# A hybrid decoder layer on one core: combinations of w_out formed during the input projection, and the down projection split between the two halves

## The chip, the cores and the metric
The kernel runs on one NeuronCore of one Trainium2 chip. A core has a matrix engine (TensorE, PE in the profile), a vector engine (VectorE, DVE), a scalar engine (ScalarE, ACT), GpSimd (POOL) and SyncE (SP), which here issues all the DMAs. Each engine takes its instructions in program order and waits on semaphores. The metric is the device time of the whole program in microseconds.

## The reference
One layer over 2048 positions of width 1024, all in float32. RMS norm, one input projection, stick-breaking attention in 8 heads of 64 beside a gated short convolution, one output projection w_out over both, residual; then RMS norm and SwiGLU with a hidden width of 2816.

```python
h = _rms_norm(x, norm_mix[l])
proj = h @ w_in[l]
q, k, v, cb, cc, cu = jnp.split(proj, splits, axis=-1)
...
mix = jnp.concatenate([attn, conv], axis=-1)
x = x + mix @ w_out[l]
h = _rms_norm(x, norm_ffn[l])
g = h @ w_gate[l]
u = h @ w_up[l]
x = x + (jax.nn.silu(g) * u) @ w_down[l]
```

## The kernel before
Each float32 matmul is made of three in a rounded format: an operand is split into a high part (ScalarE, a rounding copy) and a low part (operand minus high part, on VectorE or GpSimd), and PE does high x high, high x low and low x high.

**Input projection (`qkv_stage`).** 16 tiles of 128 tokens. PE does, per tile t, the 24 matmuls of q, the transposes of the normalized x of tile t+1 (L405) and of q and k of tile t-1 (L415), then k, then v. The root for the norm of tile t+1 is made by GpSimd (`x_rstd`, L222 and L225) at the head of its step t; VectorE scales x with it (L320) at the head of its own. GpSimd's other work in a step is the root for q and k (L236, L239). SyncE ends step t with the store of v (L203), for which it waits on `v_done`, and begins the next with x, then the transposed h. All engines meet at the end of the stage.

**Attention and convolution (`attend_conv_stage`)**, untouched, to about 1102 us.

**The back (`back_stage`)** does w_out, gate, up and down. w_out, gate and up use a Strassen-Winograd scheme: seven products P1 to P7 of blocks in place of eight. For that, operand A (tokens of mix, or weights of gate and up) and operand B (w_out; then h of one half of the tokens) are combined: A's sums on VectorE (`pair_sum`, L1623 to L1639; `sums`, L1701 to L1715), B's four combinations in `t_part` (VectorE, L1692) with one `copy` on ScalarE (L1434). B has seven regions of 1 MB (high and low part 4 x 512 columns each); `b_hi` (L1442) rounds, `b_lo` (L1222) makes the low part, on VectorE or GpSimd by `LO_ON_DVE` and `LO_ON_POOL`.
B is filled three times: with w_out (f = 0), with h of the first 1024 tokens (f = 1), with h of the other 1024 (f = 2), each time as the products before set regions free; `HOME` says which region a product's B is in. A product is 12 matmuls (L1920 to L1924).
The order: the opening (the first two pairs of token tiles, 14 products by the list `OPENING`), six more pairs of seven products (`MIX`); 11 rounds of 14 products (gate and up) for the first half, 11 for the second; then down in 4 groups of 22 chunks, 24 matmuls a chunk (L76 to L78). In a round ScalarE rounds the operands of the next round (`hi`, L1454), keeps results of PE (`keep`, L1472) and does the silu; GpSimd makes the low parts (`lo`, L1873); SyncE loads the next round's raw weights when the last low part of the round before is made (`load_raw`, L1287). The 12 loads of h for f = 2, its combinations and low parts stand in the last round of the first half and the first of the second ("the turn" below). In down, `split` (ScalarE), `wd_split` (VectorE) and `hid_split` (GpSimd) prepare the chunk ahead; down's operands lie in regions of A, its result in `s`, which the rounds use too.
The orders are written out by hand: each engine's block is one list in program order.

Of the kernel before, what the change touches and what calls it, by code (L numbers as in the profile page):

```python
# [110 lines left out]
def qkv_stage(nc, cst, x, norm_mix, w_in, q_norm, k_norm, hT_hi_dram, hT_lo_dram, qk_hi_dram, qk_lo_dram, v_dram):  # L111
# [9 lines left out]
    with ExitStack() as stack:  # L121
# [14 lines left out]
        qkT_hi, qkT_lo = m.sb("qkT_hi", [P, 2, 2 * PAIRS, P], F32R), m.sb("qkT_lo", [P, 2, 2 * PAIRS, P], F32R)  # L136
        proj = m.ps("proj", [P, 2, 3, BANK])
# [13 lines left out]
        v_stored, qkT_stored = [m.sem("v_stored0"), m.sem("v_stored1")], [m.sem("qkT_stored0"), m.sem("qkT_stored1")]  # L151
        block = m.block()
# [21 lines left out]
        def _(sp):
# [35 lines left out]
            tiles(sp, step, tail=3)  # L210
            sp.wait_ge(qkT_lo_done, 2 * TILES)
            store_qk(TILES - 1, (TILES - 1) % 2)
            for b in range(2):
                sp.wait_ge(v_stored[b], DMA * TILES // 2)
                sp.wait_ge(hT_stored[b], DMA * TILES)
                sp.wait_ge(qkT_stored[b], DMA * TILES)

        @block.gpsimd
        def _(pool):
# [22 lines left out]
            tiles(pool, step)  # L242
# [1834 lines left out]
```

## Time and profile before

| | us |
|---|---|
| median of 3 runs | 2678.88 |
| lowest and highest | 2678.44, 2680.89 |
| the profiled execution | 2681.3 |
| its span, first to last instruction | 2679.4 |
| PE busy in the span | 2510.6 |
| VectorE, GpSimd, ScalarE busy | 1349.9, 1321.9, 1164.4 |
| mean granted clock of PE | 0.974 |

The profiled execution's time is 1.9 us more than its span. The stages in it: projection to 322 us, attention and convolution to 1102, w_out from 1119 to 1318, gate and up to 2196, down to the end. A row of the timeline gives start and duration of an instruction (or of a few alike, xN), and in brackets how long its engine stood idle before it and what released it. A matmul's duration contains its pipeline; where they follow each other, the distance of the starts is what one costs.

### The profile page before, as it was taken

How to read it: one execution, taken by the hardware profiler on the slowest of the kernel's cores; microseconds unless marked ns; L12 is line 12 of the kernel's file. 1: busy time of each engine (PE TensorE's matmuls, PEld its weight loads, DVE VectorE, ACT ScalarE, POOL GpSimd, SP SyncE). 2: the span in 40 equal slices, each digit the busy share in tenths (PEclk: the TensorE clock that was granted, in tenths of full speed). 3: DMA queues.
4: the chain of work that ended last, by engine and by line, in shares of the span. 5: the costliest groups of instructions: out<-in, count | busy, mean ns of one | idle time of the engine just before them, and what ended most of it. 6: DMA issues, size and time to landing. Idle time of an engine off the chain costs nothing.

```text
span 2679.4 us, 34937 instructions
## 1 busy us (share of the span) xinstructions
PE 2510.6 (94%) x12176; PEld 2072.5 (77%) x12176; DVE 1349.9 (50%) x1377; ACT 1164.4 (43%) x1883; POOL 1321.9 (49%) x918
## 2 busy tenths in 40 slices
PE   8999779999899999579899999989999999999999
PEld 6788667777777778468778888868888888888887
DVE  4434246766667767465665454574454432222232
ACT  3222256777677677433443333343333322322222
POOL 1212156767667676465684455464455423333332
PEclk9999989999999999789999999989999999999999
DMA  5655563443533522335522222323212225555554
GB/s 173 199 177 166 160 187 99 122 113 98 144 88 103 164 68 53 134 124 206 189 95 94 82 71 82 119 85 95 94 60 84 92 90 171 186 172 183 173 189 153
DMA packets 305117, 343.93 MB, mean 128 GB/s; under 512 B 19169, under 2 KB 242401, under 8 KB 303969
## 3 DMA queue, kind: packets, MB, share of 16 engines
q1 hardware_dynamic: 304992, 342.44, 41.3%
q8 instruction: 58, 0.95, 0.1%
q14 instruction: 67, 0.54, 0.1%
HBM read 243.81 MB, written 98.57 MB: 128 GB/s over the span
## 4 chain that ended last, share of the span: by engine, by line
PE 50%; POOL 2%; DMA 1%; issue 1%; DVE 1%; ACT 1%; DVEq 0%; ACTq 0%; POOLq 0%
PE ffn_ps L1920 11%; PE ffn_ps L1924 11%; PE ffn_ps L1922 11%; PE ffn_ps L77 6%; PE ffn_ps L78 6%; PE ffn_ps L76 6%; POOL all_B L1222 1%; POOL ffn_A L1873 1%; DMA ffn_raw<-in_w_up 1%; DVE all_B_over L1692 0%; DMA ffn_s<-in_x 0%; PE ffn_ps L1950 0%; POOL ffn_A L1856 0%; ACT all_B L1442 0%; ACT ffn_A L1454 0%
## 5 line engine op out<-in xcount | busy, mean ns | idle before, releaser
L1920 PE MATMUL ffn_ps<-all_B,ffn_A 128*128 128x512 f32 x1456 | 576.9, 396 | 64.7 <-issue 18.4
L1924 PE MATMUL ffn_ps<-all_B,ffn_A 128*128 128x512 f32 x1456 | 574.0, 394 | 0.0
L1922 PE MATMUL ffn_ps<-all_B,ffn_A 128*128 128x512 f32 x1456 | 574.0, 394 | 0.0
L1873 POOL TENSOR_TENSOR ffn_A<-ffn_raw,ffn_A 128x512 fp32r<-128x512 f32 x264 | 369.1, 1409 | 379.8 <-ACT ffn_A L1454 379.6
L829 DVE TENSOR_TENSOR_SCAN att_stick<-att_z,att_stick 128x128 f32<-128x128 f32 (+5 forms) x192 | 331.3, 1726 | 220.5 <-ACT att_z L741 209.2
L875 POOL TENSOR_TENSOR att_a<-att_a,att_stick 128x128 f32<-128x128 f32 (+5 forms) x192 | 281.4, 1471 | 217.1 <-DVE att_stick L829 216.5
L1920 PEld LDWEIGHTS ffn_ps<-all_B,ffn_A 128*128 128x128 f32 x1456 | 278.1, 191 | 127.0 <-issue 52.0
L1881 POOL TENSOR_TENSOR ffn_A<-ffn_A_over,ffn_A 128x512 fp32r<-128x512 f32 x88 | 158.3, 1799 | 349.0 <-ACT ffn_A L1494 349.0
L1924 PEld LDWEIGHTS ffn_ps<-all_B,ffn_A 128*128 128x128 f32 x1456 | 277.7, 191 | 58.8
L1922 PEld LDWEIGHTS ffn_ps<-all_B,ffn_A 128*128 128x128 f32 x1456 | 278.1, 191 | 57.4
L1746 DVE TENSOR_TENSOR ffn_A<-ffn_A_over,ffn_A 128x1024 fp32r<-128x1024 f32 x88 | 107.8, 1225 | 348.3 <-ACT ffn_A L1492 348.3
L76 PE MATMUL ffn_ps<-ffn_A 128*128 128x512 f32 x704 | 273.9, 389 | 0.0
L77 PE MATMUL ffn_ps<-ffn_A 128*128 128x512 f32 x704 | 273.9, 389 | 0.0
L78 PE MATMUL ffn_ps<-ffn_A 128*128 128x512 f32 x704 | 273.9, 389 | 0.0
L1454 ACT ACTIVATE ffn_A<-ffn_raw 128x512 fp32r<-128x512 f32 x264 | 162.6, 627 | 235.0 <-PE ffn_ps L1924 88.1
L1492 ACT ACTIVATE ffn_A<-ffn_A_over 128x1024 fp32r<-128x1024 f32 x88 | 93.3, 1060 | 333.4 <-PE ffn_ps L78 326.8
L752 ACT ACTIVATE att_aT_hi<-att_tr 128x512 fp32r<-128x512 f32 (+2 forms) x320 | 158.2, 535 | 148.0 <-PE att_tr L965 146.9
L841 DVE TENSOR_TENSOR att_aT_lo<-att_tr,att_aT_hi 128x512 fp32r<-128x512 f32 (+2 forms) x320 | 180.6, 597 | 34.1 <-ACT att_aT_hi L752 33.4
L965 PE MATMUL att_tr<-all_ident,att_a 128*128 128x128 f32 x1088 | 159.5, 281 | 36.4 <-DVE att_aT_lo L841 33.5
L965 PEld LDWEIGHTS att_tr<-all_ident,att_a 128*128 128x128 f32 x1088 | 128.6, 143 | 76.3 <-issue 33.6
L1472 ACT ACTIVATE ffn_s<-ffn_ps 128x512 f32<-128x512 f32 x132 | 78.5, 596 | 224.9 <-PE ffn_ps L1924 224.8
L76 PE MATMUL att_proj<-att_hT_hi,att_w_hi 128*128 128x512 f32 x384 | 161.5, 421 | 15.3 <-ACT att_y L777 8.5
(118 smaller groups left out, 4676.6 us busy)
## 6 DMA issues: line engine op xcount, KB each, us to landing
ffn_A_over<-in_w_down SPq DMA_DIRECT2D x88, 512.0 KB, 3.5
att_w_stage<-in_w_in SPq DMA_DIRECT2D x48, 512.0 KB, 4.3
ffn_raw<-in_w_gate SPq DMA_DIRECT2D x22, 1024.0 KB, 6.9
ffn_raw<-in_w_up SPq DMA_DIRECT2D x22, 1024.0 KB, 9.0
hidT<-ffn_s SPq DMA_DIRECT2D x88, 256.0 KB, 2.4
ffn_A_over<-hidT SPq DMA_DIRECT2D x88, 256.0 KB, 3.5
qkv_x_t<-in_x SPq DMA_DIRECT2D x16, 512.0 KB, 4.5
hT_hi<-qkv_hT_hi SPq DMA_DIRECT2D x16, 512.0 KB, 5.4
```

What stands on the lines that cost most here:

```text
L76: nc.tensor.matmul(out, lhs_hi, rhs_hi, start=first, stop=False)
L77: nc.tensor.matmul(out, lhs_hi, rhs_lo, start=False, stop=False)
L78: return nc.tensor.matmul(out, lhs_lo, rhs_hi, start=False, stop=last)
L829: nc.vector.tensor_tensor_scan(stick[:, row % 2, c0:c1][:, ::-1], z[:, n % 2, 0:nb * P][:, ::-1], stick[:, row % 2, S:S + 1].to_broadcast( ...
L841: nc.vector.tensor_tensor(aT_lo[:, gi % 2, blocks, toks], tr[:, f % 2, 0:nj, :], aT_hi[:, gi % 2, blocks, toks].bitcast(F32), ALU.subtract ...
L875: nc.gpsimd.tensor_tensor(a[:, n % 4, 0:nb * P], a[:, n % 4, 0:nb * P], stick[:, row_of[n] % 2, c0:c0 + nb * P], ALU.mult).then_inc(a_done, 1)
L965: last = nc.tensor.transpose(tr[:, f % 2, i, :], a[:, n % 4, (j + i) * P:(j + i + 1) * P], cst["ident"][:, :])
L1454: nc.scalar.activation(A[:, j, p, 0, :, :], operand(j, p), ACT.Copy).then_inc(hi_done, 1)
L1873: nc.gpsimd.tensor_tensor(A[:, j, p, 1, :, :], operand(j, p), A[:, j, p, 0, :, :].bitcast(F32), ALU.subtract).then_inc(lo_done, 1)
L1920: nc.tensor.matmul(ps[:, bank_, :], A[:, j, p, 0, k, :], B[home][:, 0, k, :], start=first and k == 0, stop=False, skip_group_check=True)
L1922: nc.tensor.matmul(ps[:, bank_, :], A[:, j, p, 0, k, :], B[home][:, 1, k, :], start=False, stop=False, skip_group_check=True)
L1924: mm = nc.tensor.matmul(ps[:, bank_, :], A[:, j, p, 1, k, :], B[home][:, 0, k, :], start=False, stop=k == HK - 1, skip_group_check=True)
```

## The change
**In the projection.** SyncE loads w_out in four pieces of 1 MB, and GpSimd forms from each the four combinations that the scheme needs (four subtractions of 128x512). They are kept in DRAM (`wt_dram`, 4 MB). A piece stands at the head of steps 11 to 14 on SyncE and on GpSimd (`TAIL` = 5; in the tile's step that follows it, GpSimd's first work is `x_rstd`).
**In the opening.** B's f = 0 is loaded whole, 7 MB instead of 4: P1, P2, P3 from w_out, P5, P6, P7, P4 from `wt_dram`. The four `t_part` and the `copy` of f = 0 go; P6's low part moves from VectorE to GpSimd.
**Before the first gate round.** Raw weights of up are loaded at step NM-9 instead of NM-7, the loads of h for P7 and P3 come at NM-5 and NM-4 with exchanged regions, the last pair's operands are made two per step, and six of the eight sums of the round come in the first three of the last seven steps.
**The halves.** Down for the first 1024 tokens (groups 0 and 1, 44 chunks) stands between the first half's and the second half's rounds. B's f = 2 is loaded and prepared in those chunks: loads behind chunks 4 to 19, combinations at 23 to 29, roundings at 24 to 36, low parts at 28 to 34 (VectorE) and 38 to 42 (GpSimd). Of the second half's first round only products 0 and 1 are prepared ahead of down; the others follow down's last chunk.

```diff
@@ qkv_stage, sync
+            def piece(k):
+                if k > 0:
+                    sp.wait_ge(wt_done, 4 * k)
+                    sp.dma_start(wt_dram.rearrange("n p k c -> p n k c")[:, :, k - 1, :], wt[:, :, :]
+                                 ).then_inc(wt_stored, DMA)
+                if k < KT // 2:
+                    sp.dma_start(wo[:, :, :], w_out.rearrange("(h k p) d -> p h k d", h=2, p=P)[:, :, k, :]
+                                 ).then_inc(wo_in, DMA)
-            tiles(sp, step, tail=3)
+            tiles(sp, step, tail=TAIL, piece=piece)
@@ qkv_stage, tiles
             for t in range(TILES - tail, TILES):
+                if piece:
+                    piece(t - TILES + tail)
                 step(t, t % 2, last=t == TILES - 1)
@@ qkv_stage, gpsimd
+            def piece(k):
+                if k == KT // 2:
+                    return
+                pool.wait_ge(wo_in, DMA * (k + 1))
+                wait(pool, wt_stored, DMA * k)
+                b11, b12, b21, b22 = (wo[:, h, n * BANK:(n + 1) * BANK] for h in range(2) for n in range(2))
+                nc.gpsimd.tensor_tensor(wt[:, 0, :], b12, b11, ALU.subtract).then_inc(wt_done, 1)
+                pool.wait_ge(wt_done, 4 * k + 1)
+                nc.gpsimd.tensor_tensor(wt[:, 1, :], b22, wt[:, 0, :], ALU.subtract).then_inc(wt_done, 1)
+                nc.gpsimd.tensor_tensor(wt[:, 2, :], b22, b12, ALU.subtract).then_inc(wt_done, 1)
+                pool.wait_ge(wt_done, 4 * k + 3)
+                nc.gpsimd.tensor_tensor(wt[:, 3, :], b21, wt[:, 1, :], ALU.subtract).then_inc(wt_done, 1)
-            tiles(pool, step)
+            tiles(pool, step, tail=TAIL, piece=piece)
@@ tables
+FIRST_SUMS = SUMS[:6]
+B_AT = [24, 26, 28, 30, 32, 34, 36]
-    return dict(zip((P1, P3, P7, P5, P6, P2, P4), freed))
+    return dict(zip((P1, P7, P3, P5, P6, P2, P4), freed))
-LO_ON_POOL = [(P2, P3), (P2, P4, P3), (P2, P4, P3)]
+LO_ON_POOL = [(P2, P6, P3), (P2, P4, P3), (P2, P4, P3)]
@@ back_stage, vector, before the first gate round
+                    if k < 3:
+                        for j, p in FIRST_SUMS[2 * k:2 * k + 2]:
+                            sums(0, j, p)
                     if k == 5:
-                        sums(0, GATE, P6)
                         t_part(1, 0)
                     if k == 6:
-                        sums(0, UP, P6)
                         lo_b(1, P1)
+                        t_part(1, 1)
@@ back_stage, scalar, hi
+                if R == ROUNDS:
+                    if p in (P5, P6):
+                        act.wait_ge(tile_done, GT * (PER - 1))
+                        act.wait_ge(hid_lo_done, PER)
+                    elif p == P7:
+                        act.wait_ge(wd_lo_done, PER)
+                    elif p in (P4, P3):
+                        act.wait_ge(tile_done, GT * PER)
@@ back_stage, scalar, between the halves
+                for e in range(PER * G + 1, PER * (G + 1)):
+                    split(e)
+                    if G == 0 and e in B_AT:
+                        b_hi(2, HI_ORDER[2][B_AT.index(e)])
+                        if e == B_AT[2]:
+                            copy(2)
+                if G + 1 < HALVES:
+                    for n in range(2, NP):
+                        hi(ROUNDS * (G + 1), n)
@@ back_stage, tensor
             for G in range(HALVES):
...
-            for g in range(GROUPS):
-                chunk(CHUNKS * g, 0, g=g)
+                for q in range(HG):
+                    g = HG * G + q
+                    chunk(CHUNKS * g, 0, g=g)
```

GpSimd in the projection before: the last turn of its loop (steps 13 and 14) and step 15. `qkv_rstd` is the root of x, `qkv_qk_rstd` that of q and k.

```order
L222 TENSOR_TENSOR qkv_msq<-qkv_ss,all_eps 128x1 [waits qkv_ss_done]
L225 TENSOR_TENSOR qkv_rstd<-qkv_msq,all_minus_half 128x1 [waits qkv_msq_done]
L236 TENSOR_TENSOR qkv_qk_msq<-qkv_qk_ss,all_eps 128x16 [waits qkv_qk_ss_done]
L239 TENSOR_TENSOR qkv_qk_rstd<-qkv_qk_msq,all_minus_half 128x16 [waits qkv_qk_msq_done]
L167 REGISTER_ALU
L167 COMPARE_AND_BRANCH
```

GpSimd there now: the loop ends with step 10, and steps 11 and on are written out; the first two combine pieces 0 and 1.

```order
L172 COMPARE_AND_BRANCH
L267 TENSOR_TENSOR qkv_wt<-qkv_wo 128x512 [waits qkv_wo_in]
L269 TENSOR_TENSOR qkv_wt<-qkv_wo,qkv_wt 128x512 [waits qkv_wt_done]
L270 TENSOR_TENSOR qkv_wt<-qkv_wo 128x512
L272 TENSOR_TENSOR qkv_wt<-qkv_wo,qkv_wt 128x512 [waits qkv_wt_done]
L240 TENSOR_TENSOR qkv_msq<-qkv_ss,all_eps 128x1 [waits qkv_ss_done]
L243 TENSOR_TENSOR qkv_rstd<-qkv_msq,all_minus_half 128x1 [waits qkv_msq_done]
L254 TENSOR_TENSOR qkv_qk_msq<-qkv_qk_ss,all_eps 128x16 [waits qkv_qk_ss_done]
L257 TENSOR_TENSOR qkv_qk_rstd<-qkv_qk_msq,all_minus_half 128x16 [waits qkv_qk_msq_done]
L267 TENSOR_TENSOR qkv_wt<-qkv_wo 128x512 [waits qkv_wt_stored,qkv_wo_in]
```

The four subtractions stand between the root of q and k of one tile and the root of x of the tile after the next; nothing stood there before.

SyncE in the projection now, from the end of step 10 (store of v) to the head of step 12:

```order
L210 DMA v_rows<-qkv_v_out 128x1024
L172 REGISTER_ALU
L172 COMPARE_AND_BRANCH
L224 DMA qkv_wo<-in_w_out 128x2x1024
L184 DMA qkv_x_t<-in_x 128x1024 [waits qkv_xn_done]
L204 DMA hT_hi<-qkv_hT_hi 128x8x128 [waits qkv_hT_lo_done]
L204 DMA hT_lo<-qkv_hT_lo 128x8x128
L214 DMA qk_hi<-qkv_qkT_hi 128x8x128 [waits qkv_qkT_lo_done]
L214 DMA qk_lo<-qkv_qkT_lo 128x8x128
L210 DMA v_rows<-qkv_v_out 128x1024 [waits qkv_v_done]
L221 DMA wt<-qkv_wt 128x4x512 [waits qkv_wt_done]
L224 DMA qkv_wo<-in_w_out 128x2x1024
```

Before, the load of x (L177 there) followed the store of v directly. Now the load of w_out is between them, and from the second piece on the store of the combinations too.

VectorE in the opening before, from the first combination (L1692) to the last low part of B (L1222); `ffn_ps` to `ffn_s` are the sums of products:

```order
L1692 TENSOR_TENSOR all_B_over<-all_B_over 128x2048 [waits ffn_b_lo_dve,ffn_b_in1,ffn_b_in0]
L1222 TENSOR_TENSOR all_B_10889<-all_B_over,all_B_10889 128x2048 [waits ffn_t_copied,ffn_b_hi_done]
L1639 TENSOR_TENSOR ffn_raw<-ffn_raw 128x4x128 [waits ffn_m_sum_done,ffn_m_lo_done] x2
L1650 TENSOR_TENSOR ffn_s<-ffn_ps,ffn_s 128x512 [waits ffn_added,ffn_x_in0,ffn_m_prod_done]
L1692 TENSOR_TENSOR all_B_over<-all_B_over 128x2048 [waits ffn_t_copied,ffn_b_in2,ffn_t_done]
L1692 TENSOR_TENSOR all_B_over<-all_B_over 128x2048 [waits ffn_t_done]
L1692 TENSOR_TENSOR all_B_over<-all_B_over 128x2048 [waits ffn_b_lo_pool,ffn_t_done]
```

And now, with the low parts of P5, P7 and P4:

```order
L1246 TENSOR_TENSOR all_B_10985<-all_B_over,all_B_10985 128x2048 [waits ffn_b_hi_done]
L1672 TENSOR_TENSOR ffn_raw<-ffn_s_11001,ffn_raw 128x4x128 [waits ffn_m_sum_done,ffn_m_lo_done] x2
L1688 TENSOR_TENSOR ffn_s<-ffn_ps,ffn_s 128x512 [waits ffn_added,ffn_x_in0,ffn_m_prod_done]
L1688 TENSOR_TENSOR ffn_s<-ffn_ps,ffn_s 128x512 [waits ffn_added,ffn_x_in2,ffn_m_prod_done]
L1688 TENSOR_TENSOR ffn_s<-ffn_ps,ffn_s 128x512 [waits ffn_added,ffn_m_prod_done] x2
L1246 TENSOR_TENSOR all_B_10987<-all_B_over,all_B_10987 128x2048 [waits ffn_b_hi_done]
L1677 TENSOR_TENSOR ffn_raw<-ffn_raw 128x4x128 [waits ffn_m_sum_done,ffn_m_lo_done] x2
L1688 TENSOR_TENSOR ffn_s<-ffn_ps,ffn_s 128x512 [waits ffn_added,ffn_x_in1,ffn_m_prod_done]
L1688 TENSOR_TENSOR ffn_s<-ffn_ps,ffn_s 128x512 [waits ffn_added,ffn_x_in3,ffn_m_prod_done]
L1246 TENSOR_TENSOR all_B_10989<-all_B_over,all_B_10989 128x2048 [waits ffn_b_hi_done]
```

The combinations are gone and the low parts wait for the rounding alone; that of P4 stands ahead of the addition of the seventh product (before, behind it).

## Rows read from the trace of the kernel before

**Rows 1.** The page: busy us of each engine; PE's busy tenths in 40 slices.
```profile
PE 2510.6 (94%) x12176; PEld 2072.5 (77%) x12176; DVE 1349.9 (50%) x1377; ACT 1164.4 (43%) x1883; POOL 1321.9 (49%) x918
...
PE   8999779999899999579899999989999999999999
```

**Rows 2.** Stretches: length, PE, PEld, DVE, ACT, POOL busy, clock, DMA, GB/s.
```profile
228.00:302.00 74.00, 74.00 (x354) 60.96 (x353) 28.36 (x36) 19.48 (x36) 15.49 (x16) 1.00 0.54 163
1119.00:1204.00 85.00, 64.23 (x245) 50.81 (x246) 58.08 (x49) 33.48 (x41) 53.29 (x32) 0.81 0.41 148
1304.00:1384.00 80.00, 64.52 (x271) 51.44 (x270) 58.60 (x43) 41.27 (x54) 67.20 (x33) 0.92 0.38 124
...
2211.00:2278.00 67.00, 67.00 (x297) 55.48 (x296) 14.71 (x12) 18.96 (x24) 21.67 (x12) 1.00 0.54 172
...
1742.00:1809.00 67.00, 53.84 (x219) 43.09 (x218) 50.64 (x32) 32.39 (x41) 43.26 (x23) 0.90 0.26 83
```

**Rows 3.** Timeline, SyncE's queue, end of tile 13: start, duration, what.
```profile
283.45 0.34 SPq L203 DMA_DIRECT2D v_rows<-qkv_v_out  x1
283.83 0.43 SPq L197 DMA_DIRECT2D hT_hi<-qkv_hT_hi  x1
```

**Rows 4.** Timeline, GpSimd: the root of x of tile 15.
```profile
283.81 0.19 POOL L222 TENSOR_TENSOR qkv_msq<-qkv_ss,all_eps 128x1 f32<-128x1 f32 x1 [3.10 <-ACT qkv_square L249]
284.07 0.55 POOL L225 TENSOR_TENSOR qkv_rstd<-qkv_msq,all_minus_half 128x1 f32<-128x1 f32 x1
```

**Rows 5.** Timeline, VectorE and PE: tile 15 normalized, and transposed.
```profile
284.66 1.29 DVE L320 SCALAR_TENSOR_TENSOR qkv_xn<-qkv_x_t,qkv_rstd,qkv_gain 128x1024 f32<-128x1024 f32 x1 [1.24 <-POOL qkv_rstd L225]
...
287.39 0.60 PE L405 MATMUL qkv_tr_x<-all_ident,qkv_xn 128*128 128x128 f32 x4
```

**Rows 6.** Timeline, GpSimd: a subtraction of 128x512 by itself.
```profile
1175.61 1.29 POOL L1856 TENSOR_TENSOR ffn_A<-ffn_raw,ffn_A 128x512 fp32r<-128x512 f32 x1 [0.36 <-ACT ffn_A L1410]
```

**Rows 7.** DMA issues: count, KB each, median us from issue to landing.
```profile
qkv_x_t<-in_x SPq DMA_DIRECT2D x16, 512.0 KB, 4.5
...
att_v_st<-v_rows SPq DMA_DIRECT2D x8, 1024.0 KB, 5.9
...
all_B_over<-in_w_out SPq DMA_DIRECT2D x4, 1024.0 KB, 9.1
```

**Rows 8.** Timeline, PE after two idle times: first slow, first fast matmul.
```profile
1139.70 0.80 PE L1920 MATMUL ffn_ps<-all_B,ffn_A 128*128 128x512 f32 x1 [6.79 <-POOL ffn_A L1856]
...
1145.30 0.39 PE L1922 MATMUL ffn_ps<-all_B,ffn_A 128*128 128x512 f32 x1
...
1326.47 0.76 PE L1920 MATMUL ffn_ps<-all_B,ffn_A 128*128 128x512 f32 x1 [8.46 <-issue]
```

**Rows 9.** A stretch of the opening, columns as in rows 2.
```profile
1120.00:1128.00 8.00, 8.00 (x27) 6.30 (x27) 5.91 (x4) 0.72 (x1) 5.91 (x3) 0.71 1.04 398
```

**Rows 10.** Timeline, opening: VectorE's combinations, and a low part beside GpSimd's.
```profile
1142.40 9.36 DVE L1692 TENSOR_TENSOR all_B_over<-all_B_over 128x2048 f32<-128x2048 f32 x3
...
1162.48 6.16 DVE L1222 TENSOR_TENSOR all_B<-all_B_over,all_B 128x2048 fp32r<-128x2048 f32 x1
...
1161.90 4.60 POOL L1222 TENSOR_TENSOR all_B<-all_B_over,all_B 128x2048 fp32r<-128x2048 f32 x1
```

**Rows 11.** Timeline, PE: transposes behind the opening's last product.
```profile
1185.77 1.03 PE L1950 MATMUL ffn_ps<-all_ident,ffn_s 128*128 128x128 f32 x8
```

**Rows 12.** Timeline, VectorE and ScalarE before the first gate round.
```profile
1318.61 1.15 DVE L1710 TENSOR_TENSOR ffn_raw<-ffn_s,ffn_raw 128x512 f32<-128x512 f32 x1
...
1321.37 1.89 ACT L1442 ACTIVATE all_B<-all_B_over 128x2048 fp32r<-128x2048 f32 x1
...
1323.29 3.08 DVE L1222 TENSOR_TENSOR all_B<-all_B_over,all_B 128x2048 fp32r<-128x2048 f32 x1 [3.53 <-ACT all_B L1442]
```

**Rows 13.** Timeline, a round's start: raw weights issued, and first used.
```profile
1385.23 0.43 SPq L1287 DMA_DIRECT2D ffn_raw<-in_w_gate  x1
...
1392.71 0.64 ACT L1454 ACTIVATE ffn_A<-ffn_raw 128x512 fp32r<-128x512 f32 x1 [7.77 <-DMA ffn_raw<-in_w_gate]
```

More of the change, by code:

```diff
@@ L160, in full_at, with tiles @@
             return 3 * t + ((2, 3, 1)[n] if isinstance(t, int) and t == 2 else n + 1)
-        def tiles(eng, step, tail=1):
+        TAIL = 5
+        def tiles(eng, step, tail=1, piece=None):
             step(0, 0, first=True)
@@ L1313, in load_x2 @@
                 if g == 0:
-                    sp.wait_ge(hid_done, 4 * (LAST + 1))
                     for n in range(4):
-                        sp.wait_ge(hid_stored[n], DMA * (LAST + 1))
                         sp.wait_ge(x2_stored[n], DMA * TILE_PAIRS // 2)
+                if g % HG == 0:
+                    sp.wait_ge(hid_done, 4 * ROUNDS * (g // HG + 1))
+                    for n in range(4):
+                        sp.wait_ge(hid_stored[n], DMA * ROUNDS * (g // HG + 1))
                 else:
@@ L1508, in _ @@
             b_hi(0, P6)
-            for n in range(8, 14):
+            b_hi(0, P7)
+            for n in range(8, 11):
                 pair_hi(n)
-            b_hi(0, P7)
             b_hi(0, P3)
             b_hi(0, P4)
+            for n in range(11, 14):
+                pair_hi(n)
             for i in range(7, NM):
@@ L1845, in _ @@
-            for e in range(1, GROUPS * CHUNKS):
-                wd_split(e)
-                if e % CHUNKS == 0:
-                    evict(e // CHUNKS - 1)
-            evict(GROUPS - 1)
+            for G in range(HALVES):
+                for c in range(ROUNDS):
+                    R = ROUNDS * G + c
+                    last = c == ROUNDS - 1
+                    more = R < LAST
+                    ahead = more and not last
+                    if more and R:
+                        for j, p in FIRST_SUMS:
+                            sums(R + 1, j, p)
+                    total(R, GATE, C22)
+                    total(R, GATE, C11)
+                    if R == 0:
+                        for j, p in FIRST_SUMS:
+                            sums(1, j, p)
+                    elif ahead:
+                        sums(R + 1, GATE, P3)
+                    total(R, UP, C22)
+                    total(R, UP, C11)
+                    hidden(R, 0)
+                    hidden(R, 1)
+                    if ahead:
+                        sums(R + 1, UP if R else GATE, P3)
+                    hidden(R, 2)
+                    total(R, GATE, C12)
+                    if R == 0:
+                        sums(1, UP, P3)
+                    if last:
+                        wd_split(PER * G)
+                    total(R, UP, C12)
+                    hidden(R, 3)
+                for e in range(PER * G + 1, PER * (G + 1)):
+                    wd_split(e)
+                    if e % PER == CHUNKS:
+                        evict(e // CHUNKS - 1)
+                    if G == 0 and e + 1 in B_AT[:4]:
+                        t_part(2, B_AT.index(e + 1))
+                    if G == 0 and e - 4 in B_AT[:4]:
+                        lo_b(2, HI_ORDER[2][B_AT.index(e - 4)])
+                evict(HG * (G + 1) - 1)
+                if G + 1 < HALVES:
+                    for j in range(2):
+                        sums(ROUNDS * (G + 1), j, P3)
```

455 lines of the change are left out of this document (206 added, 249 removed).

## The prediction

> **What bounds the kernel now.** I read the page's busy times and slices first. TensorE (PE) is busy for 2510.6 of 2679.4 us and no other engine for more than 1349.9, so time is lost or won only where PE stands still or runs at the lower clock. PE's slices (67 us each) dip at the change from projection to attention, around 1100 to 1200, near 1320 and near 1780 [rows 1]. The stretches put sizes on them [rows 2]. In 2211 to 2278 (down) PE starts 297 matmuls in 67 us, 0.2256 us each: that is full pace. In 228 to 302 (projection tiles 11 to 14) it is busy all the time at a granted clock of 1.00: **nothing is lost there today**. From 1119 to 1204 (the opening of w_out) PE is idle for 20.8 us, from 1304 to 1384 (change to the first gate round) for 15.5 us, and in the 67 us of the turn it starts 219 matmuls where 297 fit: 78 x 0.2256 = 17.6 us lost. Three of the change's four edits aim at these places; the first goes where PE has no slack to spare.
>
> **Part 1, the combinations in the projection: a new wait on PE's path.** In tiles 11 to 14 SyncE issues one 1 MB load of w_out, but in its own program order: behind the wait on v_done of the tile before. That tile's v store goes out at 283.45 and the next issue at 283.83 [rows 3]. GpSimd waits for this load, does four 128x512 subtractions, and only then the small root of the next tile, today at 283.81 to 284.62 [rows 4]. On that root waits VectorE's normalization (284.66, 1.29 us), and on it PE's next transposes, at 287.39 [rows 5]. PE takes its work in order, so projections q of this tile are done by then and k and v stand behind those transposes. The slack is 287.39 - 285.95 = 1.4 us.
> Now with landing L: 283.83 + L + 4 x 1.29 (an alone-running GpSimd subtraction of this shape [rows 6]) + 0.81 for the root + 1.33 for the normalization = 291.1 + L. PE waits for 3.7 + L in each of the four tiles. The roots come at the same place of each tile (18.5 us apart), so one tile stands for all.
> L: 1 MB loads take 5.9 us at the median (v into the attention) to 9.1 (w_out), 512 KB ones 4.5 [rows 7]. In tile 11 only the v store is ahead: I take 6.0. In the other three a 1 MB store of the combinations is issued 0.45 us ahead of the load, 2.5 MB in flight with v: I take 9.0, beside the 9.1 of the opening, where several MB are in flight too; bounds 4.5 and 12. Sum: 9.7 + 3 x (3.7 + 0.45 + 9.0) = 49.2 us; with the bounds 34 to 60 (tile 11 at 4.5 to 8).
> The Trainium skill (SBUF — State Buffer, The DMA setup-cost knee) gives a landing as 2 us and the bytes at 436 GB/s. By it 1 MB would land in 4.4 us, and the later three would wait 7.7 us for all that is in flight; the rows of 1 MB above say it is slower here. Its sum would be 8.1 + 3 x 11.9 = 44 us, an estimate.
> **Restarts.** After 6.79 us of idle PE's granted clock is at the 1.2 GHz level: 13 matmuls at 0.43 us before the next at 0.23 [rows 8], 13 x 0.2 = 2.6 us lost. Behind the idle of 8.46 us that ends at 1326.47 [rows 8] the stretch at that level was about half as long. Four new waits: 10.4 us, bounds 5 and 11. Part 1 costs 59.6 us. Nothing hides it: while PE waits, no independent matmul stands ahead of the transposes in its queue. The last combination's store (tile 15) is far from the stage's end: nothing.
>
> **Part 2, the opening.** Gone are four 128x2048 subtractions of VectorE (2.28 us each; three of them stood for 9.36 in a row beside GpSimd's work [rows 10]) and one copy of ScalarE (1.9); the low part of P6 goes from VectorE to GpSimd (4.6 us there). Added: 3 MB of loads; the DMA engines are full there and move 398 GB/s [rows 9], so the last piece lands about 8 us later, near 1140, ahead of its use. By the new order PE's third pair of products (P5) needs B's P5 low part, free at about 1133, so the idle of 6.79 us goes. Next late: P6's low part on GpSimd (to about 1143) and then P4's: VectorE has it behind GpSimd's P3, and as the 6.16 us instruction beside GpSimd's 4.60 shows, VectorE stands until GpSimd has finished [rows 10]; the sum of P6 and so P7 waits behind it on VectorE to about 1157. From there six products to the last (n=13), 16.3 us with 2.6 for a restart: about 1176, where it now ends at 1185.8, when the second tile's transposes start [rows 11]. From there the chain through the store and the load of x up to add 15 is the same. Gain 9 us. Bounds: 3 (the loads are slower), and 28, all 20.8 us of idle and three restarts.
> The Trainium skill (SBUF — State Buffer, Who interferes with whom) says a VectorE instruction with two SBUF inputs and a reading GpSimd one exclude each other; this trace agrees (6.16 us, [rows 10]). Without that rule P4 would be ready some 4 us sooner and the gain be 13.
>
> **Part 3, the first gate round.** Raw weights for up are loaded two products earlier, the last pair's operands two per step; the six sums stand in steps 0 to 2 instead of 0 to 6. Now PE stands for the 8.46 us before 1326.47 because VectorE's second P6 sum runs till 1319.8, three of ScalarE's roundings wait for it, behind them B's P1 (1321.37), and its low part is done at 1326.4 [rows 8, 12]. All of this would be ready by PE's end of the mix at 1318: 8.5 us and 1.3 of restart go. Behind it GpSimd, busy for 67.2 of 80 us [rows 2], keeps 14 low parts and three B parts of 4.6 us or more: I give half back. Gain 5, bounds 0 and 10.
>
> **Part 4, down between the halves.** The refill of B (four subtractions, seven roundings, seven low parts) leaves the turn for the first half's down, where VectorE is busy 14.7, ScalarE 19.0, GpSimd 21.7 of 67 us and DMA for 0.54 [rows 2]. The refill brings some 18, 15 and 15 us over 130 us and 4 MB: hidden, 0 (bounds 0 and 4; a chunk's low part of hid waits for a 4.6 us B part at three chunks). The 17.6 us of the turn go. What is late next is the start of the second half: ScalarE rounds product 2 and later only when the last two chunks are through, GpSimd (12 x 1.3 us) is done about 10.8 us after down's end T, and gate's next raw load is issued at T + 9.6. It takes 7.5 us (1385.23 to 1392.71), and the rounding and then the copy of P6 stand behind it on ScalarE, 1.1 us together [rows 13]: T + 18.2, where PE wants it at T + 16.3. A stall of 1.9 us. Gain 15.7, bounds 8 and 18.
>
> **Sum** against the profiled execution (2681.3 us, span 2679.4): 2681.3 + 59.6 - 9 - 5 - 15.7 = 2711.2. Its time stands 2.4 above the median of the three runs (2678.9), so the median after is about 2709.
>
> **Rivals.**
> A, *quick landings*: the four loads land in 4.5 to 6.5 us although a store is ahead. For: DMA has a share of 0.54 there [rows 2]. Against: the 1 MB rows above. Part 1 is then about 4 x 9.5 + 8 = 46: 2695.
> B, *landings queue up* behind store, v and hT: 12 us in three tiles, and x of the next tile late as well: part 1 near 70, 2720.
> C, *the turn's stall moves*: the second half starts with ScalarE blocked on raw weights, and GpSimd's catching up repeats in the next product: 10 us instead of 1.9. Against: VectorE and GpSimd have nothing else there. 2717.
> D, the other side, *the opening freed whole*: PE runs from 1119 without a gap, because no B part waits for another engine and the second tile's chain shrinks with it. It gives 28 us instead of 9, and since raw weights then come with no contention, part 3 gives 10. For: the opening idles for 20.8 us. Against: GpSimd has more to do there than before. It decides only from a gain in parts 2 to 4 above part 1; with 28 + 10 + 18 = 56 and part 1 at A's 46: 2669, faster. With part 1 as forecast it would be 2683, within what can't be told from no change.
> That part 1 wouldn't add a wait at all is excluded: even with L at nought, 3.7 us remain in each tile.
>
> **Chances.** Forecast (2700 to 2716) 0.5, A 0.2, B 0.12, C 0.1, D 0.08. About 0.2% (5 us) is what a measurement can tell from no change. Faster by more: 0.05 (most of D), within: 0.03 (the rest of D and A's edge), slower: 0.92. The range leaves out D and B's far end: 2687 to 2726.
>
> **What would show it.** In the new profile: in four tiles of the projection PE idles for 9 to 15 us ahead of the transposes of the next tile (L405 in the kernel before), released by VectorE's normalization, and GpSimd idles before its first subtraction for the w_out load; low clock after each. The opening's last product ends about 10 us nearer to its start, the wait at 1326 is gone, PE counts 297 matmuls per 67 us through gate to down, and the start of the second half shows a gap of about 2 us. I am wrong if those projection waits add up to under 40 us, or if parts 2 to 4 give over 45.

## The result, and the profile after

The changed kernel takes 2711.61 us (median of 4 runs, 2710.22 to 2712.71) against 2679.63 us for the kernel before on the same chip. The ratio is 1.0119 by the medians, 1.0116 by the paired comparison with a 95% interval of 1.0103 to 1.0129. It is slower by 32 us (1.2%), clear of the noise, and the forecast was 2709.

The page of the changed kernel (busy us of each engine, PE's busy tenths in 40 slices of 68 us):

```profile
PE 2510.4 (93%) x12176; PEld 2072.0 (76%) x12176; DVE 1340.8 (49%) x1372; ACT 1163.2 (43%) x1882; POOL 1331.4 (49%) x935
...
PE   8997658999989999959989999999999999999999
```

Against [rows 1] PE has the same 2510 us of work in a span 29.6 us longer. The fourth to the seventh slice (203 to 474 us) read 7, 6, 5, 8, where two slices read 7. The opening is a 5 followed by a 9, no longer by a 7, and the 8 of the turn (1742 to 1809) is gone.

The stretches after; columns: from:to, length, busy us of PE, PEld, DVE, ACT, POOL with counts, granted clock, DMA share, GB/s:

```profile
228.00:302.00 74.00, 45.86 (x194) 36.87 (x192) 14.18 (x18) 10.97 (x21) 17.68 (x16) 0.84 0.50 162
1179.60:1264.60 85.00, 68.94 (x286) 55.33 (x287) 48.97 (x49) 34.69 (x44) 54.55 (x37) 0.90 0.58 209
1364.00:1444.00 80.00, 70.61 (x299) 56.27 (x298) 60.67 (x40) 37.82 (x51) 60.42 (x30) 0.96 0.33 112
...
1742.00:1809.00 67.00, 67.00 (x297) 55.50 (x296) 31.09 (x33) 20.64 (x34) 22.15 (x17) 1.00 0.30 89
```

In the projection PE starts 194 matmuls in the 74 us in which it started 354 [rows 2], at a clock of 0.84 instead of 1.00. In the 85 us from the opening's first product on it is idle for 16.1 us instead of 20.8, and in the 80 us around the first gate round for 9.4 instead of 15.5. The stretch 1742 to 1809, where PE was short of 78 matmuls, now counts the full 297. Between 1430 us and the end PE waits only twice, 0.6 and 2.1 us.

Ahead of the transposes of x PE now waits five times for VectorE's normalization, 59.7 us in all. One of the five is the start of the kernel (10.0 us; 10.3 in the kernel before). The four new ones stand in PE's timeline below and add up to 49.7 us. Ahead of them, the chain that leads to the second, in the timelines of SyncE's queue, GpSimd and VectorE:

```profile
259.85 0.34 SPq L210 DMA_DIRECT2D v_rows<-qkv_v_out  x1
260.24 0.43 SPq L221 DMA_DIRECT2D wt<-qkv_wt  x1
260.72 0.92 SPq L224 DMA_DIRECT2D qkv_wo<-in_w_out  x1
...
269.55 1.26 POOL L267 TENSOR_TENSOR qkv_wt<-qkv_wo 128x512 f32<-128x512 f32 x1 [12.46 <-DMA qkv_wo<-in_w_out]
...
274.94 0.55 POOL L243 TENSOR_TENSOR qkv_rstd<-qkv_msq,all_minus_half 128x1 f32<-128x1 f32 x1
...
275.52 1.29 DVE L352 SCALAR_TENSOR_TENSOR qkv_xn<-qkv_x_t,qkv_rstd,qkv_gain 128x1024 f32<-128x1024 f32 x1 [15.70 <-POOL qkv_rstd L243]
...
243.20 1.11 PE L437 MATMUL qkv_tr_x<-all_ident,qkv_xn 128*128 128x128 f32 x4 [11.06 <-DVE qkv_xn L352]
276.94 1.11 PE L437 MATMUL qkv_tr_x<-all_ident,qkv_xn 128*128 128x128 f32 x4 [12.95 <-DVE qkv_xn L352]
310.50 1.11 PE L437 MATMUL qkv_tr_x<-all_ident,qkv_xn 128*128 128x128 f32 x4 [12.62 <-DVE qkv_xn L352]
344.77 1.11 PE L437 MATMUL qkv_tr_x<-all_ident,qkv_xn 128*128 128x128 f32 x4 [13.03 <-DVE qkv_xn L352]
```

Read it down: v goes out, then the store of the combinations, then the load, which lands 8.8 us after its issue (260.72 to 269.55; a landing here is the time from the issue to the first instruction of GpSimd that uses the data). Four subtractions of 1.26 us follow, then the root that [rows 4] had at the end of the v store, then the normalization, then PE. The transposes take 1.11 us for four where [rows 5] has 0.60: the granted clock from 276.90 to 281.50 is 0.50, the 1.2 GHz level. From one v store to the next it is now 33.8 us (259.85 to 293.68), where it was 18.4. The v stores also measure the whole part. Here are the last one ahead of the four tiles and the last of the projection, first in the kernel before and then in the changed one:

```profile
228.09 0.34 SPq L203 DMA_DIRECT2D v_rows<-qkv_v_out  x1
319.46 0.34 SPq L203 DMA_DIRECT2D v_rows<-qkv_v_out  x1
...
228.08 0.34 SPq L210 DMA_DIRECT2D v_rows<-qkv_v_out  x1
379.31 0.34 SPq L210 DMA_DIRECT2D v_rows<-qkv_v_out  x1
```

From 91.4 us the time between them has gone to 151.2: the projection costs 59.9 us more.

The opening: PE's first product in the kernel before, then PE's larger idle times in the changed kernel, and the GpSimd and VectorE rows behind the largest:

```profile
1119.16 0.76 PE L1920 MATMUL ffn_ps<-all_B,ffn_A 128*128 128x512 f32 x1 [17.07 <-DVE all_B L1222]
...
1179.77 0.76 PE L1955 MATMUL ffn_ps<-all_B,ffn_A 128*128 128x512 f32 x1 [16.29 <-DVE all_B L1246]
1202.15 0.47 PE L1955 MATMUL ffn_ps<-all_B,ffn_A 128*128 128x512 f32 x1 [2.76 <-issue]
1216.55 0.76 PE L1955 MATMUL ffn_ps<-all_B,ffn_A 128*128 128x512 f32 x1 [7.11 <-DVE ffn_s L1688]
...
1209.14 4.51 POOL L1246 TENSOR_TENSOR all_B<-all_B_over,all_B 128x2048 fp32r<-128x2048 f32 x1
...
1210.70 5.10 DVE L1246 TENSOR_TENSOR all_B<-all_B_over,all_B 128x2048 fp32r<-128x2048 f32 x1 [2.60 <-ACT all_B L1475]
1215.73 0.68 DVE L1688 TENSOR_TENSOR ffn_s<-ffn_ps,ffn_s 128x512 f32<-128x512 f32 x1
...
1235.72 1.03 PE L1985 MATMUL ffn_ps<-all_ident,ffn_s 128*128 128x128 f32 x8
```

From the first product to the transposes behind the last it is 56.0 us (1179.77 to 1235.72) instead of 66.6 (1119.16 to 1185.77 [rows 11]). PE waits till 1202.15 for P6's low part on GpSimd, and P4's ends at 1215.8 on VectorE, beside GpSimd's P3 (the 4.51 us row); the sum for product 6 stands behind it and PE idles 7.11 us.

PE at the first gate round and at the start of the second half, and ScalarE's copies of results (`keep`) there, after:

```profile
1369.54 0.47 PE L1955 MATMUL ffn_ps<-all_B,ffn_A 128*128 128x512 f32 x1 [0.89 <-issue]
...
1423.83 0.47 PE L1955 MATMUL ffn_ps<-all_B,ffn_A 128*128 128x512 f32 x1 [3.21 <-DVE ffn_s L1766]
...
2054.29 0.47 PE L1955 MATMUL ffn_ps<-all_B,ffn_A 128*128 128x512 f32 x1 [2.14 <-ACT ffn_s L1515]
...
2053.57 1.06 ACT L1515 ACTIVATE ffn_s<-ffn_ps 128x512 f32<-128x512 f32 x2
2060.21 0.58 ACT L1515 ACTIVATE ffn_s<-ffn_ps 128x512 f32<-128x512 f32 x1
```

The 8.46 us of [rows 8] have become 0.89. The smaller waits behind it have grown: they add up to 8.4 us up to 1424, where they were 6.6. The second half begins with a stall of 2.14 us, 8.3 us behind down's end (2043.83).

### The profile page after: what moved, and what is told of

Read it like the earlier page. It is cut to its first block, busy times and chain, and to the rows that moved or that the text cites. A ratio compares the mean times of both kernels' runs of the same rounds, so it can differ in the third digit from the quotient of the medians.

```text
span 2709.0 us, 34956 instructions
## 1 busy us (share of the span) xinstructions
PE 2510.4 (93%) x12176; PEld 2072.0 (76%) x12176; DVE 1340.8 (49%) x1372; ACT 1163.2 (43%) x1882; POOL 1331.4 (49%) x935
## 4 chain that ended last, share of the span: by engine, by line
PE 51%; DVE 1%; POOL 1%; DMA 1%; issue 1%; ACT 0%; SPq 0%; DVEq 0%; ACTq 0%
PE ffn_ps L1955 11%; PE ffn_ps L1957 11%; PE ffn_ps L1959 11%; PE ffn_ps L77 6%; PE ffn_ps L76 6%; PE ffn_ps L78 6%; POOL ffn_A L1895 1%; PE ffn_ps L1985 0%; DMA ffn_s<-in_x 0%; DVE all_B L1246 0%; DVE ffn_raw L1729 0%; DMA ffn_A_over<-hidT 0%; DVE ffn_raw L1739 0%; DVE all_B_over L1716 0%; DMA h2T<-ffn_s 0%
## 5 line engine op out<-in xcount | busy, mean ns | idle before, releaser
L1955 PE MATMUL ffn_ps<-all_B,ffn_A 128*128 128x512 f32 x1456 | 573.0, 394 | 40.9 <-DVE all_B L1246 18.4
L1751 DVE TENSOR_TENSOR ffn_s<-ffn_ps,ffn_s 128x512 f32<-128x512 f32 x132 | 90.4, 689 | 178.2 <-PE ffn_ps L1959 112.5
```

Of the source, the lines that this page charges most:

```text
L1955: nc.tensor.matmul(ps[:, bank_, :], A[:, j, p, 0, k, :], B[home][:, 0, k, :], start=first and k == 0, stop=False, skip_group_check=True)
```

## Experiments

Each kernel was compared with the kernel before on the same chip; "+" and "-" below are against that kernel's median of the same call (2678.92 for the first four runs, 2679.06 for the other four). The changed kernel stands at +32.0.

**The root ahead of the subtractions** (e1_root_first). GpSimd's step, with nothing else changed:

```
             def step(t, b, first=False, last=False):
                 if not last and not normed(t + 1):
                     x_rstd(t + 1, 1 - b)
+                if isinstance(t, int) and t >= TILES - TAIL:
+                    piece(t - TILES + TAIL)
...
-            tiles(pool, step, tail=TAIL, piece=piece)
+            tiles(pool, step, tail=TAIL)
```

> The changed kernel, but in a tile's step of the projection GpSimd takes the root of the next tile's normalization first and the three subtractions of a w_out row behind it. Theory (the 49.4 us of TensorE's new waits and the restarts exist because the root stands behind the wait for the w_out load and behind the subtractions): the projection goes back to its period of before, four waits of 11 to 13 us go, the time falls by about 59.6 us to 2652 us, 27 us below the kernel before. Rival (the 12 MB of added DMA traffic and GpSimd's subtractions themselves slow the projection, wherever they stand): at least half of the loss stays, over 2680 us.

(There are four subtractions to a row, not three, and of the added traffic 8 MB lie in the projection.) Measured: 2651.31 us, -27.6, ratio 0.9898 [0.9883, 0.9913]. So the place of the root costs 32.0 + 27.6 = 59.6 us. The rival falls: the same loads, stores and subtractions, in the same tiles, now cost PE next to nothing. A stretch of the root-first kernel, GpSimd in its last such tile, and the last v store:

```profile
228.00:302.00 74.00, 73.88 (x352) 60.59 (x352) 26.17 (x34) 19.73 (x36) 32.92 (x31) 1.00 0.82 263
...
284.89 0.55 POOL L243 TENSOR_TENSOR qkv_rstd<-qkv_msq,all_minus_half 128x1 f32<-128x1 f32 x1
296.51 1.29 POOL L269 TENSOR_TENSOR qkv_wt<-qkv_wo 128x512 f32<-128x512 f32 x1 [11.06 <-DMA qkv_wo<-in_w_out]
...
320.01 0.34 SPq L210 DMA_DIRECT2D v_rows<-qkv_v_out  x1
```

PE starts 352 matmuls where 354 were started before, although the DMA engines are at 0.82 and 263 GB/s. GpSimd waits 11.06 us for this load, about as long as in the changed kernel (10.4 to 12.5), but PE no longer waits for GpSimd. The v stores (228.33 and 320.01) are 91.7 us apart, against 151.2 in the changed kernel: 59.6 us in the traces too.

**The load a tile earlier** (e2_load_early). GpSimd keeps the changed kernel's order; the rows alternate between two buffers, and the store of the combinations moves as well, to the place that it has in the next experiment:

```
-                pool.wait_ge(wo_in, DMA * (k + 1))
+                pool.wait_ge(wo_in[k % 2], DMA * (k // 2 + 1))
...
-            tiles(sp, step, tail=TAIL, piece=piece)
+            tiles(sp, step, tail=TAIL + 2, piece=piece)
...
-            tiles(pool, step, tail=TAIL, piece=piece)
+            tiles(pool, step, tail=TAIL + 2, piece=piece)
```

> The changed kernel with GpSimd's order kept (subtractions ahead of the root), but the w_out row is loaded one tile earlier into a second buffer and the combinations are stored as soon as they are formed. Theory (of the loss per tile, 3.7 us are the three subtractions and their start and the other 7 to 9 us the wait for the load; with the load away only what exceeds the slack is left): PE's wait in each of the four tiles falls from 11 to 13 us to 0.5 to 3 us and no longer lets the clock fall, about 2655 us (2652 to 2664). Rival (the subtractions, beside VectorE, are the expensive part): 2680 us or more.

Measured: 2654.03 us, -24.9, ratio 0.9903 [0.9889, 0.9917]. PE and GpSimd in the second of the four tiles, timeline:

```profile
248.82 0.55 POOL L253 TENSOR_TENSOR qkv_rstd<-qkv_msq,all_minus_half 128x1 f32<-128x1 f32 x1
...
250.82 0.65 PE L447 MATMUL qkv_tr_x<-all_ident,qkv_xn 128*128 128x128 f32 x4 [0.59 <-DVE qkv_xn L362]
```

The subtractions still stand ahead of the root, and PE waits 0.6 to 0.7 us in each tile, with no slow matmuls behind. With the row at hand they begin right behind the q and k roots, in GpSimd's idle time, not behind the v store. So the cost comes from the landing, which starts to count only behind the v store and pushes the subtractions behind it too. (Two things were moved here; the next run moves the store alone.)

**The store of the combinations earlier** (e5_store_early):

```
+                k = t - TILES + TAIL if isinstance(t, int) else -1
+                if 0 <= k < KT // 2:
+                    sp.wait_ge(wt_done, 4 * (k + 1))
+                    sp.dma_start(wt_dram...[:, :, k, :], wt[:, :, :]).then_inc(wt_stored, DMA)
                 if not first:
                     sp.wait_ge(qkT_lo_done, 2 * t)
                     store_qk(t - 1, 1 - b)
...
-                if k > 0:
-                    sp.wait_ge(wt_done, 4 * k)
-                    sp.dma_start(wt_dram...[:, :, k - 1, :], wt[:, :, :]).then_inc(wt_stored, DMA)
```

> The changed kernel, but the combinations of a w_out row are stored in the step that forms them, ahead of the q and k stores, not in the next step; the load stays where it is. Theory (the first landing takes 7.0 us and the next three 8.4 to 8.8 us because the 3 MB store of the combinations is issued just ahead of the load): the three later waits fall by 1.8 us of landing and 0.45 us of issue each, 6.8 us together, 2705 us. Rival (the landing doesn't depend on the store ahead of it, and the early store only delays the q and k stores): within 2 us of 2711.6.

(The store is 1 MB, not 3.) Measured: 2700.75 us, +21.8, ratio 1.0080 [1.0066, 1.0093]: 10.2 us regained, 3.4 more than expected. SyncE's queue and GpSimd in the second tile:

```profile
258.37 0.43 SPq L225 DMA_DIRECT2D qkv_wo<-in_w_out  x1
...
264.82 1.26 POOL L268 TENSOR_TENSOR qkv_wt<-qkv_wo 128x512 f32<-128x512 f32 x1 [9.58 <-DMA qkv_wo<-in_w_out]
```

The landing takes 6.4 us here instead of 8.8, and PE's four waits are 9.81, 10.11, 9.83 and 10.30, 40.1 us instead of 49.7. The landing does depend on what is issued just ahead of it: the three later ones are 6.1 to 6.6 us here, and 8.4 to 9.3 in all fifteen cases where the store is just ahead (the changed kernel and the four others that keep its loads and stores). Part of the miss of the expectation is the first tile, whose landing has no such store ahead in any of these kernels: it took 7.0 us in the changed kernel and 5.7 to 6.2 in the five others, so the 7.0 that the expectation started from was a high one.

**The wait ahead of the root, the subtractions behind** (e8_wait_then_root), on top of the root-first kernel:

```
+                if isinstance(t, int) and TILES - TAIL <= t < TILES - 1:
+                    pool.wait_ge(wo_in, DMA * (t - TILES + TAIL + 1))
                 if not last and not normed(t + 1):
                     x_rstd(t + 1, 1 - b)
```

> The changed kernel, but GpSimd waits for the w_out row, then takes the root, and only then the four subtractions: the wait for the landing stays in front of the root, the subtractions don't. Theory (the wait per tile is a sum of landing and subtractions less the slack): TensorE waits about 4.5 + 3 x 7.9 = 28 us in the four tiles instead of 49.4, and each wait still ends in a stretch at the lower clock: 2651.3 + 28 + 8 to 10 = 2688 to 2690 us. Rival 1 (waits of 5 to 8 us no longer lower the clock): 2679 us. Rival 2 (the subtractions run beside other work of GpSimd that is waited for anyway): over 2700 us.

Measured: 2689.34 us, +10.3, ratio 1.0037 [1.0023, 1.0051]: inside the theory's 2688 to 2690. PE's four waits and the last v store, timelines:

```profile
237.72 1.11 PE L441 MATMUL qkv_tr_x<-all_ident,qkv_xn 128*128 128x128 f32 x4 [5.61 <-DVE qkv_xn L356]
...
266.24 1.11 PE L441 MATMUL qkv_tr_x<-all_ident,qkv_xn 128*128 128x128 f32 x4 [8.44 <-DVE qkv_xn L356]
...
295.69 1.11 PE L441 MATMUL qkv_tr_x<-all_ident,qkv_xn 128*128 128x128 f32 x4 [8.39 <-DVE qkv_xn L356]
...
325.06 1.11 PE L441 MATMUL qkv_tr_x<-all_ident,qkv_xn 128*128 128x128 f32 x4 [9.26 <-DVE qkv_xn L356]
...
359.19 0.34 SPq L210 DMA_DIRECT2D v_rows<-qkv_v_out  x1
```

They add up to 31.7 us, where 28 were expected; against root-first the time is 37.9 us longer (27.6 + 10.3), which leaves 6.2 us for four restarts, where 8 to 10 were expected. That the sum came out to the microsecond is luck: the waits were 4 us longer and the restarts cheaper. The v stores, free of what varies elsewhere in the kernel, say 39.5 us (228.06 to 359.19, against 91.7) and 7.8 us for four. In the changed kernel the four waits are 49.7 and the difference 59.6, by medians and by v stores alike: 9.9 us for four. All eight waits end in slow transposes (1.11 us); behind them 19 projection matmuls run slow here and 29 in the changed kernel.

**The other edits alone.** The first kernel here is the kernel before with only B's refill moved into down (e3_down_only); the second also has the sums of the first gate round moved up (e4_down_and_gate). Both take the combinations and the opening back, among others:

```
-            tiles(sp, step, tail=TAIL, piece=piece)
+            tiles(sp, step, tail=3)
...
-LO_ON_POOL = [(P2, P6, P3), (P2, P4, P3), (P2, P4, P3)]
+LO_ON_POOL = [(P2, P3), (P2, P4, P3), (P2, P4, P3)]
...
-LOADS = [(P1, P2, P5, P6, P7, P3, P4), (P1, P7, P3, P2), (P1, P7, P3, P2)]
+LOADS = [(P1, P7, P3, P2), (P1, P7, P3, P2), (P1, P7, P3, P2)]
```

and the second against the first, in GpSimd's, ScalarE's and VectorE's programs alike (here ScalarE's), with SyncE's loads for it earlier:

```
-                if i + 7 < NM:
+                if i + 14 < NM:
...
+                elif i + 7 < NM:
+                    for n in range(2 * (i % 7), min(2 * (i % 7) + 2, 7)):
+                        pair_hi(NM - 7 + n)
```

> The kernel before with the fourth edit alone: B's refill moved from the turn between the halves into the first half's down. Theory: the turn's 17.6 us go and a stall of about 2 us at the start of the second half comes, 14.5 us less than before as the changed kernel's trace has it (15.7 by the prediction): 2664 to 2665 us. Rival (the gain seen in the changed kernel's trace is partly that of other edits, or the refill costs down something): 2668 us or more.

> The third and fourth edit together, without the combinations formed in the projection and without the new opening. Theory: a further 5 to 6 us below the kernel with the fourth alone, about 2659 us; then the root-first kernel (2651.3), which adds the first two edits without their wait, puts the new opening at 8 us (9 by the prediction, 10.7 by the trace). Rival (the sums of the first gate round only gain when the opening before them is the new one): the same as the fourth edit alone, 2664 to 2665 us, and the opening is worth 13 us.

Measured: 2666.15 us, -12.9, ratio 0.9949 [0.9936, 0.9963]; and 2658.50 us, -20.6, ratio 0.9921 [0.9908, 0.9935]. The fourth edit works alone, and the third with the fourth alone. So the fourth edit is worth 12.9, the third 20.6 - 12.9 = 7.7, the second, with the first's work but not its wait, 27.6 - 20.6 = 7.0, and the first costs 59.6. (That the four add up to the 32.0 is no test: they are taken as differences along one chain of kernels.) Each of these is a difference of medians whose intervals are some 4 us wide on either side, so the split between the small ones is soft. The traces are sharper there. PE at the first product and at the transposes behind the last, in the kernel with the third and fourth edit:

```profile
1117.49 0.77 PE L1968 MATMUL ffn_ps<-all_B,ffn_A 128*128 128x512 f32 x1 [16.66 <-DVE all_B L1254]
...
1183.05 1.04 PE L1998 MATMUL ffn_ps<-all_ident,ffn_s 128*128 128x128 f32 x8
```

and in the root-first kernel, with its idle times between:

```profile
1120.45 0.76 PE L1957 MATMUL ffn_ps<-all_B,ffn_A 128*128 128x512 f32 x1 [17.63 <-DVE all_B L1248]
...
1142.79 0.76 PE L1957 MATMUL ffn_ps<-all_B,ffn_A 128*128 128x512 f32 x1 [2.75 <-issue]
1157.20 0.77 PE L1957 MATMUL ffn_ps<-all_B,ffn_A 128*128 128x512 f32 x1 [7.36 <-DVE ffn_s L1690]
...
1177.16 1.03 PE L1987 MATMUL ffn_ps<-all_ident,ffn_s 128*128 128x128 f32 x8
```

65.6 us without the new opening and 56.7 with it: 8.9 us. The start of the opening itself wanders by up to 3 us between the traces (1117.5 to 1120.5), and this blurs the times.

**The sum for product 6 ahead of P4's low part** (e6_add6_first), on top of root-first:

```
+            add(6)
             lo_b(0, P4)
-            add(6)
```

> e1_root_first, and in the opening behind attention VectorE forms the sum for product 6 ahead of its piece of the low part of B's P4 (now that piece of 5.10 us stands in front, and TensorE idles 7.11 us for the sum). Theory (TensorE's wait there is for the order on VectorE): 6 to 8 us less than e1_root_first, about 2645 us. Rival (the work is needed right after by the next products anyway, and the wait only moves to them): the same as e1_root_first within 2 us.

Measured: 2647.07 us, -31.9, ratio 0.9881 [0.9865, 0.9896]: 4.2 us less than root-first by medians. PE in this kernel:

```profile
1140.19 0.69 PE L1957 MATMUL ffn_ps<-all_B,ffn_A 128*128 128x512 f32 x1 [2.75 <-issue]
1151.87 0.47 PE L1957 MATMUL ffn_ps<-all_B,ffn_A 128*128 128x512 f32 x1 [1.64 <-issue]
1158.04 0.77 PE L1957 MATMUL ffn_ps<-all_B,ffn_A 128*128 128x512 f32 x1 [3.18 <-DVE ffn_s L1690]
```

The 7.36 us have become 1.64 and 3.18: part of the wait was the order on VectorE, and part came back at the next sums, which P4's low part now holds up. The traces give the edit less than the medians do. From the first product (1117.87) to the transposes (1172.92) it is 55.1 us, where root-first takes 56.7: 1.7 us. Another 2.6 us of the difference between the two traces lie ahead of the opening, where both kernels have the same instructions. So of the 4.2 us only 1.7 are shown to be the edit's, which is the rival's size and not the 6 to 8 us of the theory. This kernel has the lowest median of all measured here.

**P6's low part first** (e7_p6_first), on top of that:

```
+            b_hi(0, P6)
             pair_hi(6)
             pair_hi(7)
-            b_hi(0, P6)
             b_hi(0, P7)
...
-            for n in range(4, 8):
+            for n in range(4, 6):
                 pair_lo(n)
             lo_b(0, P6)
-            for n in range(8, 11):
+            for n in range(6, 11):
```

> The root-first kernel with add 6 ahead (e6_add6_first), and B's P6 rounded by ScalarE and its low part taken by GpSimd ahead of the first tiles' operands for products 6 and 7. In e6 TensorE stands 2.75 us at 1137.4 until GpSimd's low part of P6 (1135.54, 4.55 us) ends, and its clock falls. Theory: the low part ends 4 us sooner, the stall and its restart go, 3 to 4 us less than e6: 2643 us. Rival (the raw row of P6 isn't there sooner, or the next operand is late instead): within 1.5 us of 2647.

Measured: 2648.96 us, -30.1, ratio 0.9891 [0.9876, 0.9907], the same as without: the theory's 3 to 4 us didn't come. GpSimd and VectorE in this kernel:

```profile
1132.86 5.13 POOL L1248 TENSOR_TENSOR all_B<-all_B_over,all_B 128x2048 fp32r<-128x2048 f32 x1 [1.49 <-ACT all_B L1477]
...
1133.44 5.89 DVE L1674 TENSOR_TENSOR ffn_raw<-ffn_s,ffn_raw 128x512 f32<-128x512 f32 x2
```

and the same two in the kernel without it:

```profile
1135.54 4.55 POOL L1248 TENSOR_TENSOR all_B<-all_B_over,all_B 128x2048 fp32r<-128x2048 f32 x1
...
1131.51 1.47 DVE L1674 TENSOR_TENSOR ffn_raw<-ffn_s,ffn_raw 128x512 f32<-128x512 f32 x2
```

Counted from PE's first product (1119.81 here, 1117.87 there) the low part did end 4 us sooner, and PE's stall of 2.75 us for it is gone. But it now runs beside two VectorE sums, which take 5.89 us instead of 1.47; ScalarE's rounding and GpSimd's low part of the next operand wait for them, and PE stands 1.22 us for that operand:

```profile
1140.61 0.50 PE L1957 MATMUL ffn_ps<-all_B,ffn_A 128*128 128x512 f32 x1 [1.22 <-POOL ffn_A L1880]
```

Its next stall, for a sum on VectorE, is 3.08 us instead of 1.64, and the opening takes 55.4 us (55.1 without the edit). It is the second half of the rival, the next operand late, and the exclusion that [rows 10] show is how: it doesn't go away when GpSimd's piece moves, it meets another VectorE instruction.

## Why the prediction was right

- **Part 1, the wait.** Forecast 49.2 us, measured 49.7. The landings were 7.0, 8.8, 8.5 and 8.9 us, where 6.0 and three times 9.0 stood in the sum. The 1 MB rows [rows 7] were the right price, and the store issued just ahead is what lifts it (6.4 us on average without, e5_store_early). By the Trainium skill (SBUF — State Buffer, The DMA setup-cost knee) a 1 MB landing would be 4.4 us, an estimate; the shortest seen in these kernels' projections was 5.7 us.
- **Part 1, the structure.** "3.7 + L" counted the root as standing behind both landing and subtractions. e8_wait_then_root takes the subtractions out of the path and e2_load_early the landing, and both times fell inside what this addition had given for them, the first of them with two misses that cancel.
- **Restarts.** 10.4 forecast, 9.9 measured (59.6 - 49.7). The total is right and its make-up is not: the forecast had 13 slow matmuls of 0.2 us behind each wait, and the trace has 6 to 8; some 1.1 us of each restart are in the eight transposes and the first matmul behind them, which the sum had left out. Part 1 as a whole: 59.6 forecast, 59.6 between the changed and the root-first kernel; that the last digit agrees is luck.
- **Part 2.** Gain 9; 10.7 in the trace of the changed kernel, 8.9 between e4_down_and_gate and e1_root_first, 7.0 by medians. The stall forecast behind VectorE's P4 is the one at 1216.55, and e6_add6_first shows that little of it was due to the order (1.7 us in the trace). By the Trainium skill (SBUF — State Buffer, Who interferes with whom) the two engines exclude each other on such subtractions; the 5.10 us beside GpSimd's 4.51 agree.
- **Part 3.** Gain 5. The raw load of the second round is issued at 1429.34 instead of 1385.23, 44.1 us later, while the transposes behind the opening are 49.95 later: 5.8 in the trace, 7.7 by medians. Half had been given back to GpSimd's load. In the trace the waits behind the first product grew by 1.8 us and end at ScalarE's and VectorE's instructions or at none that the profile shows; that GpSimd's load is their cause isn't shown.
- **Part 4.** Gain 15.7, measured 14.5 in the trace of the changed kernel (44.1 us late at the second round's load, 29.6 at the end) and 12.9 alone. The turn is whole (297 matmuls), the refill in down costs one wait of 0.6 us and the new stall is 2.14 us where 1.9 was forecast. That these sizes agree is luck, for it is another wait. The forecast had PE waiting 16.3 us behind down's end for a copy of P6 that stands behind gate's raw load. That load landed in 5.5 us and not in 7.5, the copy was done at 2060.8, 17.0 us behind down's end, and PE, by then 2.1 us late, didn't wait for it. The stall that did come stands at 8.3 us and is for the copies that start at 2053.57, which stand on ScalarE behind a rounding at 2053.03; it waits for a sum of VectorE (2051.24), and this for a low part of GpSimd. The rows give 17.6 - 0.6 - 2.1 = 14.9. The trace of the edit alone gives 16.1 (1.4 us earlier than before at the second round's load, 17.5 at the end), its median 12.9; they differ by what the runs vary.
- **The sum.** The traces give 60.6 us more up to the opening's first product (59.9 of them in the projection), and 10.7, 5.8 and 14.5 less behind it: the 29.6 us by which the span grew. The forecast had 59.6, 9, 5 and 15.7.
- **The rivals.** A needed landings of 4.5 to 6.5 us behind a store and did not happen; even with the store out of the way (e5_store_early) they are 6.1 to 6.6 and the time is 2700.75, above A's 2695. B and C did not happen either. D needed an opening freed whole; it gained 7 to 11 of 28 us, held back by P6 on GpSimd and P4 on VectorE, as the text of part 2 has it.

## What to carry to other kernels

Before putting filler work on an engine with idle time, look at the smallest instruction behind it in that engine's order and who waits for it: here one root of 0.55 us behind a load decided 60 us, and moving it ahead turned a loss of 32 us into a gain of 28. A filler that waits for a DMA belongs behind what the critical engine needs, or its load must be issued early enough that the filler starts in the idle time. When the bottleneck engine is stopped, price the wait plus its restart at the lower clock: here some 2 us behind waits of 6 to 9 us and 2.5 behind waits of 11 to 13.

## What the runs showed of the hardware that was not expected

- A load issued 0.5 us behind a 1 MB store landed 8.5 to 8.9 us after its issue, and 6.1 to 6.6 in the same tiles without the store: some 2.3 us, though the DMA engines' share over 228 to 302 us was only 0.50 in the first case.
- DMA traffic of 263 GB/s at a share of 0.82 beside the projection took nothing from PE (352 matmuls against 354).
- The restart at the lower clock is not one fixed price (projection matmuls of 0.55 us or more, where full pace has 0.39): behind idle times of 5.6, 8.4, 8.4 and 9.3 us, 2, 8, 3 and 6 projection matmuls ran slow; behind 11.1 to 13.0 us it was 6 to 8. Idle times of 0.6 to 0.7 us (e2_load_early) showed none.
- Two VectorE sums of 128x512 took 5.89 us instead of 1.47 beside one GpSimd subtraction of 128x2048.
